# Seven block products in place of eight in most of two MLPs, with the hidden tiles kept in DRAM

## The reference

```python
hdn = jnp.einsum('bsd,df->bsf', rms_norm(x, mlp_norm_g[l]), w_up[l])   # block two
hdn = jnp.square(jax.nn.relu(hdn))
x = x + jnp.einsum('bsf,fd->bsd', hdn, w_down[l])

def squared_relu_mlp(x, w1, w2):                                       # block three
    return jnp.square(jax.nn.relu(x @ w1)) @ w2
x = layer_norm_3(ALPHA * x + squared_relu_mlp(x, w_ff1[l], w_ff2[l]), ln2_g[l], ln2_b[l])
```

## Time and profile before

| | |
|---|---|
| median of 3 runs | 3630.79 us (3630.08 to 3631.36) |
| profiled execution, first to last instruction | 3628.6 us |
| PE busy | 3583.7 us, 99% |
| DVE, ACT, POOL busy | 1738.8, 1151.8, 1118.1 us (48%, 32%, 31%) |
| granted TensorE clock, mean | 0.996 |
| moved by DMA | 229.41 MB, mean 63 GB/s |

### The profile page before, as it was taken

How to read it: one execution, slowest core, us unless ns; L and a number is a source line. 1 busy time by engine, 2 the same in 40 slices (tenths; PEclk the granted TensorE clock), 3 DMA queues, 4 the chain that set the end, 5 groups by cost and what they waited for, 6 DMA issues and landing times.

```text
span 3628.6 us, 43938 instructions
## 1 busy us (share of the span) xinstructions
PE 3583.7 (99%) x18494; PEld 2958.3 (82%) x18494; DVE 1738.8 (48%) x2289; ACT 1151.8 (32%) x1490; POOL 1118.1 (31%) x748
## 2 busy tenths in 40 slices
PE   8999999999999999999999999999999999999997
PEld 7999878888888878887888888877887788888886
DVE  6667509999544563344522222227667732222226
ACT  6555422222421434442311111125333421111113
POOL 4444312222343431113522222225113532222223
PEclk9999999999999999999999999999999999999998
DMA  3110121111332331102211111113112211111112
GB/s 113 30 36 30 42 82 56 56 59 53 111 134 93 105 125 31 44 24 99 87 48 47 47 47 47 47 58 125 35 41 82 76 59 47 47 50 49 47 47 76
DMA packets 65141, 229.41 MB, mean 63 GB/s; under 512 B 7217, under 2 KB 7473, under 8 KB 64945
## 3 DMA queue, kind: packets, MB, share of 16 engines
q1 hardware_dynamic: 64944, 226.60, 18.9%
HBM read 201.40 MB, written 25.17 MB: 62 GB/s over the span
## 4 chain that ended last, share of the span: by engine, by line
PE 91%; DVE 6%; ACT 1%; issue 1%; POOL 0%; DMA 0%; SPq 0%; DVEq 0%; ACTq 0%
PE psum L536 81%; PE psum L692 1%; PE psum L990 1%; PE psum L957 1%; PE psum L972 1%; PE psum L637 1%; PE psum L717 0%; PE psum L716 0%; DVE hl L2189 0%; DVE k L3019 0%; PE psum L708 0%; DVE h L2996 0%; DVE h L2984 0%; DVE bs L2986 0%; DVE den L2978 0%
## 5 line engine op out<-in xcount | busy, mean ns | idle before, releaser
L3318 POOL TENSOR_TENSOR wl<-raw,wh 128x512 fp32r<-128x512 f32 x636 | 890.4, 1421 | 2249.9 <-ACT wh L1327 2249.9
L536 PE MATMUL psum<-hh,wh 128*128 128x512 f32 (+2 forms) x3760 | 1200.2, 390 | 13.1 <-POOL wl L3318 9.2
L536 PE MATMUL psum<-hh,wl 128*128 128x512 f32 (+2 forms) x3760 | 1159.7, 379 | 0.0
L536 PE MATMUL psum<-hl,wh 128*128 128x512 f32 (+2 forms) x3760 | 1154.7, 378 | 0.1
L536 PEld LDWEIGHTS psum<-hh,wh 128*128 128x128 f32 x3760 | 677.3, 188 | 155.9 <-issue 32.0
L536 PEld LDWEIGHTS psum<-hl,wh 128*128 128x128 f32 x3760 | 693.2, 188 | 132.7 <-DVE hl L2189 0.6
L536 PEld LDWEIGHTS psum<-hh,wl 128*128 128x128 f32 x3760 | 694.4, 188 | 127.1
L1327 ACT ACTIVATE wh<-raw 128x1024 fp32r<-128x1024 f32 x318 | 335.2, 1054 | 762.8 <-PE psum L536 762.2
L536 PE MATMUL psum<-hdh,wh 128*128 128x512 f32 x1024 | 334.0, 398 | 5.0 <-DVE B L3219 4.4
L536 PE MATMUL psum<-hdl,wh 128*128 128x512 f32 x1024 | 331.2, 396 | 0.0
L536 PE MATMUL psum<-hdh,wl 128*128 128x512 f32 x1024 | 331.2, 395 | 0.0
(11 more groups left out here) (443 smaller groups left out, 2855.9 us busy)
## 6 DMA issues: line engine op xcount, KB each, us to landing
raw<-in_wts SPq DMA_DIRECT2D x318, 512.0 KB, 3.6
keep_x<-B SPq DMA_DIRECT2D x14, 512.0 KB, 5.8
X<-in_xin SPq DMA_DIRECT2D x8, 520.0 KB, 5.2
keep_sz<-tmp SPq DMA_DIRECT2D x8, 512.0 KB, 2.9
tmp<-keep_sz SPq DMA_DIRECT2D x8, 512.0 KB, 3.8
av<-keep_gr SPq DMA_DIRECT2D x8, 512.0 KB, 3.4
av<-keep_gc SPq DMA_DIRECT2D x8, 512.0 KB, 3.5
xc<-keep_x SPq DMA_DIRECT2D x8, 512.0 KB, 5.4
```

What stands on the lines that cost most here:

```text
L536: ins = pe.matmul(out, w, x[:, k, c0:c0 + width], start=first and n == only[0], stop=final and n == only[-1])
L3318: gp.tensor_tensor(wl[:, s, a], raw[:, s, a], fp(wh[:, s, a]), SUB).then_inc(*c.lo.tick(i, p))
```

## The change

Of each MLP, the first 4 hidden tiles are computed as before. For the other 28 hidden tiles the two matrix products are done by Strassen's scheme. The matrices are cut in 2x2 blocks: tokens in two halves of 512, input features in two halves of 4 tiles, hidden features in 14 pairs of tiles. Seven products of sums of blocks stand in place of eight products of blocks.

**Ups.** For pair j of hidden tiles and Strassen product p, one `product` is 12 matmuls of 128x512 into one PSUM bank (4 input tiles x 3). There are 14 x 7 = 98 of them, in the order 2, 4, 5, 3, 1, 7, 6. The sums of input tiles are made once per MLP on DVE (`in_sums`: five sums of four 128x512 tiles, each with a hi part on ACT and a lo part on DVE). The sums of weight blocks are made for each product that needs one (5 of 7, `w_add`, 128x512 on DVE); ACT makes the hi part (`w_high`), POOL the lo part, in rings of four blocks. DVE puts the 2x2 hidden blocks together from PSUM (`hidden`), with two of them first copied by ACT (`copy_out`), squares them, and makes the five sums that the down products will need. All seven inputs, 256 KB each, are stored in DRAM (`HD`).

**Downs.** After all ups, seven passes, one for each Strassen product in the order 3, 5, 1, 6, 4, 2, 7; each pass has 14 steps, and each step loads one stored input (256 KB), splits it (`act_high` on ACT, `act_low` on DVE), and does 12 matmuls into the 4 banks of the pass (4 output tiles x 3). After a pass, each of its 4 banks is added to or subtracted from one or two blocks of X (`fold`). Passes 3 and 1 also load diagonal weight blocks that stay in SBUF; passes 5, 6, 2 and 7 load one 256 KB weight block per step.

**Room.** The new buffers lie over others: the norm before block two's MLP now writes in place over X, X itself is stored in DRAM before that (`xm2`, and `xm3` in block three) and loaded again during the first down pass (`xl`). The squares of the first 4 hidden tiles are stored in DRAM as well (`HT`) and loaded in the sixth pass, for the down slabs of the first group, which now come last.

```diff
-GATES3, POOL3, OUT3, MLP3 = 210, 231, 235, 247
-NSLAB = 318
+GATES3, POOL3, OUT3, MLP3 = 154, 175, 179, 191
+NSLAB = 206
+PAIRS = 14
+NUP, NFAST = 7 * PAIRS, 14 * PAIRS
+UP_ORDER = (2, 4, 5, 3, 1, 7, 6)
+DOWN_ORDER = (3, 5, 1, 6, 4, 2, 7)
...
 def tensor():
+        def fast_mlp(base):
+            for n in range(NUP):
+                p, x = fast_product(n), up_bank(base, n)
...
+                elif n >= 8:
+                    pe.wait_ge(*up_free(base, n - 8))
+                if n < 7 and p in IN_SUM:
+                    pe.wait_ge(*c.in_lo(base, p))
+                pe.wait_ge(*c.w_hi(base, n))
+                (xh, xl), a, b = IN[p], w_ring(wh, base, n), w_ring(wl, base, n)
+                for w, y in ((a, xh), (a, xl), (b, xh)):
+                    if w is b:
+                        pe.wait_ge(*c.w_lo(base, n))
+                    for k in range(4):
+                        ins = pe.matmul(x, w[:, k * 128:(k + 1) * 128], y[:, k, :], start=(w is a and y is xh and k == 0),
+                                        stop=(w is b and k == 3))
+                ins.then_inc(*c.fast.tick(base, n))
+            for pi in range(7):
+                for t in range(PAIRS):
...
+                            ins = pe.matmul(down_bank(base, pi, j), w[:, j * 128:(j + 1) * 128], y,
+                                            start=(t == 0 and w is a and y is xh), stop=(t == PAIRS - 1 and w is b))
...
 def scalar():
+        def fast_mlp(base):
+            for n in range(NFAST):
+                w_high(base, n)
+                if n == 1:
+                    in_highs(base, 3)
+                elif n == 3:
+                    in_highs(base, 6)
+                m = n - NUP
+                if 4 <= n < NUP + 4 and fast_product(n - 4) in (2, 5):
+                    copy_out(base, n - 4)
+                if m >= 0:
+                    act_high(base, m)
+                if 0 <= m - 5 * PAIRS - 4 < 8:
+                    first_high(base, m - 5 * PAIRS - 4)
...
 def vector():
+        def fast_mlp(base):
+            for u in range(4):
+                squared(base, u, 0)
+            for u, p in enumerate((4, 1, 7)):
+                in_sums(base, p)
+                squared(base, u, 1)
...
+            in_sums(base, 3)
+            in_sums(base, 6)
+            for n in range(NFAST):
+                w_add(base, n + 5)
+                m, t = n - NUP, (n - NUP) % PAIRS
+                if m >= -3 and m + 3 < NFAST - NUP:
+                    act_low(base, m + 3)
+                if m < 0:
+                    hidden(base, n)
+                if m >= PAIRS and t in (1, 3, 5, 7):
+                    fold(base, m // PAIRS - 1, t // 2)
...
 def gpsimd():
+        def fast_mlp(base):
+            split(base + 7)
+            for n in range(NFAST):
+                gp.wait_ge(*c.w_hi(base, n))
+                gp.tensor_tensor(w_ring(wl, base, n), w_src(base, n), fp(w_ring(wh, base, n)), SUB).then_inc(*c.w_lo.tick(base, n))
...
 def sync():
+            for m in range(6):
+                down_step(base, m)
+            keep_pair(base, PAIRS - 1)
+            for m in range(6, NFAST - NUP):
+                down_step(base, m)
+                if m == 6:
+                    for j in (PAIRS - 2, PAIRS - 1):
+                        for p in range(1, 8):
+                            sp.wait_ge(*c.kept(base, p, j))
+                if 6 <= m < PAIRS:
+                    k = m - 6
...
+                    load(("xl", base, k), X[:, k, :], XS[k])
```

More of the change, by code:

```diff
@@ new lines, in tail_ready, with whole_downs @@
+        def tail_ready(base, k):
+            for hf in range(2):
+                pe.wait_ge(*c.a_lo("first", base, k, hf))
+        def whole_downs(base):
+            for j in range(HALVED[base]):
+                i, prs = down_at(base, j), [None, None]
+                for e, k in DOWN_FIRST if j == 0 else DOWN_REST:
+                    if k == 0:
+                        prs[e] = grab(pairs, (i, e), c.ev_v("dn", base, 7, 2 * j + e))
+                    if j == 0 and e == 0:
+                        tail_ready(base, k)
+                    ins = three(prs[e], None, i, k, 4 * e + k, k == 0, k == 3, hdh, hdl, 0)
+                    if k == 3:
+                        ins.then_inc(*c.gemm.tick(i, e))
@@ new lines, in w_add @@
+        def w_add(base, n):
+            if n >= NFAST or fast_product(n) not in W_SUM:
+                return
+            p = fast_product(n)
+            a, op, b = W_SUM[p]
+            if n < NUP:
+                for z in range(2):
+                    ve.wait_ge(*c.block("up", base, n // 7, z))
+            else:
+                for mk in (a, b):
+                    ve.wait_ge(*(c.block("cache", base, mk, (n - NUP) % PAIRS) if mk[0] == mk[1] else c.block("one", base, n)))
+            q = SUMMED.index(n)
+            if q > 3:
+                ve.wait_ge(*c.w_lo(base, SUMMED[q - 4]))
+            ve.tensor_tensor(w_src(base, n), w_block(base, n, a), w_block(base, n, b), op).then_inc(*c.w_sum.tick(base, n))
@@ new lines, in fold @@
+        def fold(base, pi, j):
+            p = DOWN_ORDER[pi]
+            ve.wait_ge(*c.fast("bank", base, pi, j))
+            if pi:
+                ve.wait_ge(*fold_done(base, pi - 1, 3))
+            for z, (mt, op) in enumerate(FOLDS[p]):
+                x = out_block(mt, j)
+                if FIRST_FOLD[mt] == p:
+                    ve.wait_ge(*c.loaded("xl", base, 4 * mt[0] + j))
+                if FIRST_FOLD[mt] == p and base == MLP3:
+                    ins = ve.scalar_tensor_tensor(x, x, ALPHA, down_bank(base, pi, j), MUL, op)
+                else:
+                    ins = ve.tensor_tensor(x, x, down_bank(base, pi, j), op)
+                ins.then_inc(*c.post.tick("fold", base, pi, j, z))
@@ L3657, in sync @@
             load(("xb", m), xb_of(m), XS[m])
-            if m != 2 and m != 3:
-                fetch(OUT2 + m + (3 if m == 1 else 1))
+            if m == 1:
+                fetch(OUT2 + 4)
+        for q in range(12):
+            m, hf = (q, ()) if q < 4 else (4 + q % 4, ((q - 4) // 4,))
+            sp.wait_ge(*c.ev_v("x2", m, *hf))
+            store(("xm2", m, *hf), side_of(XS[m], *hf) if hf else XS[m], side_of(X[:, m, :], *hf) if hf else X[:, m, :])
+            fetch(OUT2 + q + 4)
+        fast_mlp(MLP2, "xm2")
         fetch(GATES3 + 4)
```

609 lines of the change are left out of this document (447 added, 162 removed).

## The result

| | before | after |
|---|---|---|
| median of four runs each, us | 3631.07 (3630.08 to 3632.36) | 3542.96 (3540.15 to 3544.51) |
| ratio, with its 95% interval | | 0.9757 (0.9743 to 0.9771) |
| profiled execution, span | 3628.6 | 3540.4 |
| matmuls | 18494 | 17822 |

The kernel is 2.4% faster, 88 us where 127 were forecast: 39 us slower than the 3504 forecast, inside the range of 3484 to 3550, outside the 3490 to 3518 that stood beside it.

A forecast was written before the change was run, and what follows sets the result against it. PE was taken to bound the kernel, busy 3583.7 of 3628.6 us. 3628.6 − 156.4 + (11 + 13) + 2 × 3 = 3502.2 us of span, 3504 with the runs' median 2.2 above span; range 3484 to 3550.

The forecast's parts named there:

- What goes: Both MLPs: slabs of 48 matmuls become products of 12 at unchanged pitch; gain 78.2 us per MLP, 156.4 in all.
- rival E: Matmul pitch rises because 12 in a row share a bank; at + 2% 22 us, 3526; chance 0.05.
- Ups and downs at nothing: Fast ups and downs: DVE and POOL contention costs PE 0; bounds 101 us for ups, 78 for downs.
- A: Ups: DVE with POOL sets the pace, 28 us more, 3532; with the full 101, 3605; chance 0.20.
- D: Ups and downs: contention and latency add up, slower than before, 179 us more, 3683; chance 0.03.
- The start of the fast part: First fast products of each MLP: late input and weight sums cost 11 and 13 us; ends 3 and 20 each.
- they take turns: DVE instructions with two SBUF inputs and POOL's alternate: 1.78 us for DVE's beside POOL, against 0.68 with POOL idle.
- the signs that I named: Among them: PE waits on weight hi parts only in each fast part's first 40 us; DVE near 75% in ups.
- rival B: Starts of the fast parts and ups-to-downs handovers cost their upper bounds: 34 us more, 3538; chance 0.12.
- something else: The rest: a cause outside the forecast and the named rivals costs the time; no size given; chance 0.03.
- From ups to downs: Transition in each MLP: 1 us for DVE's late lo part, 2 for X loads; 3 us per MLP (0 to 12).
- Other edits at nothing: Norm in place and last downs: hidden, cost nothing; the norm's store, if uncovered, 3 us once.

The follow-up runs named there:

- sums_twice: Changed kernel with each weight sum in the ups made twice, a wait between: 3611.61 us, 68.6 us more than the changed kernel.
- port_arrival: No kernel computation: DVE runs of 24 additions, one POOL addition arriving behind the 1st to 20th; unbroken, with waits, or every fourth reading PSUM: 992.97 us.
- yield_to_pool: Changed kernel with DVE waiting for POOL's weight part before the input sums of products 7 and 6: 3527.99 us, 15.0 us less than the changed kernel.
- spread_loads: Changed kernel with the eight loads of X issued every second down step, 6 to 20, in order of need: 3537.34 us, 5.6 us less.
- fetch_early: Changed kernel with the last first-group up slabs asked for one store earlier by SP: 3542.30 us, ratio 0.9754 to before.
- port: No kernel computation: DVE runs of 14 additions, unbroken, with waits or with PSUM reads, one POOL addition beside each: 938.36 us.

## Why the prediction was right and where it was wrong

**What goes: right.** 336 matmuls fewer in each MLP, 78.0 us at the pitch of 0.232 that the fast ups and downs keep (1176 matmuls of L1226 from 1810.69 to 2092.97, with 7.9 us of waits up to 1826.2, 1.7 of lower clock behind them and no wait after). No rise from 12 in a row into one bank: rival E is out.

**Ups and downs at nothing: right, by a smaller margin than I wrote.** 19.50 us per pair, no wait of PE in the other 27 pairs nor in passes 2 to 7, so A and D are out. DVE is busy for 87% there, not for the 75% that I gave; by sums_twice the spare is about 1.1 us per pair. What I argued, that POOL pushes DVE back, costs DVE time, but POOL is also held back itself, and it has 9 us to spare of 19.5 (busy for 10.47).

**The start of the fast part: the step that failed.** I took 11 and 13 us and had 20 as the end of the range; it is 22 and 29. I followed it with "they take turns", which the rows had shown only for the shorter runs of the kernel before. Five sets of eight additions with a square between are long unbroken runs from SBUF, and there POOL is shut out. PE's waits for POOL in these places are 7.6 + 6.4 us in block two and 11.7 + 6.4 in block three, 32.1 of the 51.5. The mechanism is shown by port_arrival and by yield_to_pool; how much of the 32.1 it is, is known only in part: yield_to_pool gave back 15.0 us, and where it put its waits 2.2 and 0.4 us over the pitch stay in block two, for POOL's own work takes time too. Of the signs that I named, this one was wrong: PE was to wait on weight hi parts, and it waits 2.9 us on these and 14.0 on lo parts in block two.

The order that I gave held in its first part: the fast products start within 2 us of the last half slab's end; but that end itself is 11 us late, and the second delay comes inside the first products. My mark for rival B was a first fast product over 10 us behind the last half slab. Behind the kernel's own last half slab it is 1.7 us; behind the place where that lay before (1796.5), 12.5 us with the 1.7 of the start taken off. B's price, 3538, is nearly the time, and that is luck: B had 40 us for the two starts and 24 for the two transitions, where 51.5 and 8.6 came, and nothing for the 13.9 outside of the MLPs. The range was wide for A and B, and neither came; that the time lies in it is owed to this width. What came was nearest to "something else", which I had given 0.03.

A number to mend: the eight stores that I took at about 12 us are 10.6 us at 397 GB/s, which moves no term.

**The clock: missed.** Behind PE's four longest waits in the two starts the granted clock is lower for some microseconds. Windows of the kernel after, behind the waits that end at 1826.17 and at 2882.39:
```profile
1826.00:1830.00 4.00, 3.83 (x10) 3.06 (x11) 2.16 (x2) 1.12 (x2) 4.00 (x4) 0.58 0.00 0
...
2882.00:2886.00 4.00, 3.61 (x9) 2.87 (x10) 0.00 (x0) 0.00 (x0) 3.95 (x4) 0.50 1.03 384
2886.00:2890.00 4.00, 4.00 (x16) 3.24 (x15) 0.00 (x0) 0.00 (x0) 0.00 (x0) 0.82 0.83 262
```
A pitch is 0.43 us there in place of 0.232, about twice: the lower of the two levels, 1.2 GHz, for most of the window. Each 4 us at 0.58 costs 1.7. That is 9 us in the four places, by the clock of such windows and no run of its own. A fifth place is in block three's downs: behind the wait of 2.1 us that ends at 3218.52 the clock is 0.57 for 4 us and costs 1.5, and behind the same wait in block two (2130.81) it stays at 1.00.

**From ups to downs: right in size.** 4.3 us per MLP against 3. One half is DVE's late lo part, as I wrote, the other the X loads beside the weight slabs at 404 GB/s, as I wrote too; spread_loads shows the second, and that the order of the loads is part of it.

**Other edits at nothing: wrong by 13.9 us.** I priced the norm in place and the last downs and did not look at what the MLP hands on. The `only` and `freed` of the ring belong to the change; before, the ring went on with four banks. It is outside of both MLPs, which is why no row that I had chosen showed it.

## What to carry to other kernels

When a change moves a resource to new work (banks, buffers), compare what the stage behind it gets back, not only what the changed stage needs. Before DVE is given a long row of additions beside POOL's, look at which places of the row POOL's instructions will fall, and put waits at which DVE really stops, or work that reads PSUM, between them: in yield_to_pool POOL's results came 5.4 and 6.0 us earlier by this. A wait that is already met does not help: between 1789.25 and 1800.77 the program has one before each subtraction (`in_hi`) and before each square, DVE passes them all without a pause, and POOL stays out. And a stall found in a trace is worth its length only if nothing behind it ends at a fixed time: in block two fetch_early took one away for nothing.

## What the runs showed of the hardware

Two inputs from SBUF on both engines, 128x512 fp32: a POOL addition that arrives in the third to sixth instruction of an unbroken run of DVE's takes its turn (1.26 to 1.82 us in port and port_arrival, and one of DVE's 1.75 in place of 0.69); from the seventh on it waits for the end of the run, 11.90 us in the longest case, with a run of 24. A semaphore wait that stops DVE between its instructions, or one that reads PSUM, lets it in. A PSUM read does so for itself alone and does not start the count afresh: POOL, when it arrived in the ninth instruction, behind the read in the eighth, waited 2.88 us for the next (785.01), while in the fifth, behind the read in the fourth, it took its turn in 1.67. That fp32 additions meet at all agrees with the Trainium skill's "GPSIMD Engine Reference" (opening table, SBUF interfaces). The note on DVE perf modes in its "Advanced Engine Details and Errata", which I had read as leaving them out, names the two-port modes alone, but the same page names two SBUF inputs too, under "GPSIMD Details". In this kernel PE waits 32 us at the places where POOL is shut out. Whether the border at six moves with the width of the instructions was not tried. One row of the kernel before hints at it: at 967.41 POOL came in the seventh of a run of 128x1024 from SBUF, counted with the instruction in which the two had met, and was through in 1.46 us.
